# A decoder layer with product-key experts: one more raw weight buffer and half-row gather buffers in the first expert stage, a third pair buffer in the second

## The reference, cut to what matters

```python
def peer(a, w_q, k1, k2, u_exp, v_exp):        # 512 tokens, D = 2048, 8 heads, 16384 experts
    ...                                        # the routing: 16 experts and 16 gates per token and head
    def one(args):
        a_c, e_c, g_c = args
        u_sel = jnp.take(u_exp, e_c, axis=0)
        h = jnp.einsum('bthkd,btd->bthk', u_sel, a_c, preferred_element_type=jnp.float32)
        w = (g_c * jax.nn.gelu(h)).astype(a_c.dtype)
        v_sel = jnp.take(v_exp, e_c, axis=0)
        return jnp.einsum('bthk,bthkd->btd', w, v_sel)
```

## Time and profile before

| | |
|---|---|
| median of 3 runs | 2978.49 us (2977.01 to 2980.55) |
| profiled execution, its own time | 2979.05 us |
| its span in the profile | 2977.3 us |
| PE busy | 2923.9 us, 98% |
| DVE busy | 2259.8 us, 76% |
| POOL busy | 1440.4 us, 48% |
| ACT busy | 1268.4 us, 43% |
| moved by DMA | 843 MB, 283 GB/s on average |

### The profile page before, as it was taken

The page is one execution under the profiler, slowest core; times in us unless marked ns, Lnnn a source line. Parts: engine busy times, 40 slices in busy tenths (PEclk is TensorE's granted clock), DMA queues, the critical chain, the costliest instruction groups (busy, mean ns, idle before and its releaser), DMA issues.

```text
span 2977.3 us, 43219 instructions
## 1 busy us (share of the span) xinstructions
PE 2923.9 (98%) x16888; PEld 2739.3 (92%) x16888; DVE 2259.8 (76%) x2836; ACT 1268.4 (43%) x1898; POOL 1440.4 (48%) x859
## 2 busy tenths in 40 slices
PE   9999999999999999999999999999999999999998
PEld 7888668889999999999999999999999999999787
DVE  5466664578888877877787769888888889998545
ACT  5224541333333433333333344555555555566522
POOL 1012000008888778888888235443445778772000
PEclk9999999999999999999999999999999999999999
DMA  8469422235555599999999889999999999998222
GB/s 299 169 238 331 142 85 99 99 110 128 139 125 130 140 343 358 373 361 358 372 341 361 320 350 408 411 417 418 415 417 415 417 413 416 417 395 314 92 93 98
DMA packets 195807, 843.09 MB, mean 283 GB/s; under 512 B 66780, under 2 KB 87276, under 8 KB 116556
## 3 DMA queue, kind: packets, MB, share of 16 engines
q0 software_dynamic: 104592, 413.77, 37.9%
q1 hardware_dynamic: 72336, 404.83, 36.0%
q10 hardware_dynamic: 18732, 22.59, 2.2%
HBM read 768.01 MB, written 73.06 MB: 282 GB/s over the span
## 4 chain that ended last, share of the span: by engine, by line
PE 66%; DVE 13%; DMA 11%; POOL 5%; issue 3%; ACT 2%; SPq 0%; DVEq 0%; ACTq 0%; POOLq 0%
PE ps L1838 21%; PE ps L1836 21%; PE ps L1837 21%; DMA pair_in<-pair 7%; DVE wL L1110 4%; DVE rows L1617 3%; POOL pair_in L612 2%; DVE hT L1629 2%; POOL rows L597 1%; POOL rows L605 1%; DMA rows<-u_rows,idx_s 1%; DVE b_acc L1634 1%; ACT wH L656 1%; DMA rows<-v_rows,idx_b 1%; DMA raw<-s_v 1%
## 5 line engine op out<-in xcount | busy, mean ns | idle before, releaser
L1836 PE MATMUL ps<-aH,wH 128*128 128x344 f32 (+2 forms) x3088 | 1057.4, 342 | 6.3 <-DVE wL L1110 6.3
L1838 PE MATMUL ps<-aH,wL 128*128 128x344 f32 (+2 forms) x3088 | 1055.4, 342 | 0.0
L1837 PE MATMUL ps<-aL,wH 128*128 128x344 f32 (+2 forms) x3088 | 1047.1, 339 | 0.0
L565 POOL DMA_INDIRECT pair<-gates_r,idx_d x384 | 740.5, 1928 | 376.7 <-DVE gates_r L1525 242.5
L1110 DVE TENSOR_TENSOR wL<-raw,wH 128x2048 fp32r<-128x2048 f32 x333 | 778.1, 2337 | 183.2 <-ACT wH L656 180.8
L656 ACT ACTIVATE wH<-raw 128x2048 fp32r<-128x2048 f32 x333 | 636.3, 1911 | 591.5 <-PE ps L1838 538.6
L1836 PE MATMUL ps<-actH,wH 128*128 128x344 f32 x2048 | 656.7, 321 | 14.3 <-DVE wL L1110 13.8
L1838 PE MATMUL ps<-actH,wL 128*128 128x344 f32 x2048 | 656.1, 320 | 0.0
L1837 PE MATMUL ps<-actL,wH 128*128 128x344 f32 x2048 | 651.6, 318 | 0.0
L1836 PEld LDWEIGHTS ps<-aH,wH 128*128 128x128 f32 x3088 | 578.5, 187 | 47.1 <-DVE wL L1110 5.8
L1837 PEld LDWEIGHTS ps<-aL,wH 128*128 128x128 f32 x3088 | 580.6, 188 | 38.8 <-issue 1.0
(11 more groups left out here) (288 smaller groups left out, 2626.7 us busy)
## 6 DMA issues: line engine op xcount, KB each, us to landing
raw<-s_pu SPq DMA_DIRECT2D x128, 1024.0 KB
raw<-s_pv SPq DMA_DIRECT2D x128, 1024.0 KB
pair<-zeros POOLq DMA_DIRECT2D x44, 1024.0 KB, 8.7
pair_in<-pair SPq DMA_DIRECT2D x128, 348.0 KB
pair<-ut ACTq DMA_DIRECT2D x128, 172.0 KB
raw<-s_out SPq DMA_DIRECT2D x16, 1024.0 KB
raw<-s_pq SPq DMA_DIRECT2D x16, 1024.0 KB
raw<-s_gate SPq DMA_DIRECT2D x16, 1024.0 KB
```

The source lines that it names most:

```text
L565: pool.indirect_dma_start(out=gates_flat, out_offset=bass.IndirectOffsetOnAxis(ap=idx_d[0:m, t, c:c + 1], axis=0), in_=gates_r[0:m, t, c:c ...
L1836: mm(out, wh, xh, start=start, stop=False, skip_group_check=skip_group_check)
L1837: mm(out, wh, xl, start=False, stop=False, skip_group_check=skip_group_check)
L1838: return mm(out, wl, xh, start=False, stop=stop, skip_group_check=skip_group_check)
```

## The change

First stage: a fifth raw buffer, so that chunks 36 to 119 rotate through three; chunk 38 waits for a_tok_ready, as raw4 lies where gain_row did. The buffers of rows become eleven halves of 8 KB. The joined array uv_rows is gone: every pick has a gather_u and a gather_v of its own, each with its buffer and semaphore. The u halves of the first 64 picks use two buffers, the v halves three. POOL's loop is gather_u, two adds, gather_v, two adds. U_PICKS goes from 64 to 68, so that 64 picks are spread over the slots 36 to 117, four over the last eight, and 97 over the second stage.

Second stage: pair_in has three buffers, and SP issues each late chunk load one value load earlier. On ACT weight_hi comes before the weigh_pick of the slot.

```diff
-U_PICKS, LATE = 64, 4
+U_PICKS, LATE = 68, 4
...
+def halves_of(j):
+
+    if j < U_PICKS - LATE:
+        return j % 2, 2 + j % 3
+    if j < U_PICKS:
+        return 4, 2 + j % 2
+    if j <= MAIN:
+        return (5, 6) if (MAIN - j) % 2 else (7, 8)
+    return 9, 10
...
+FIRST_THIRD, END_THIRD = ROUTE_U + 4, KEYS - GROUP
...
+    if FIRST_THIRD <= c < END_THIRD:
+        return (0, 1, 4)[(c - FIRST_THIRD) % 3]
...
+def pair_at(c):
+
+    return c % 2 if c < GROUP else (c - GROUP) % 3
...
-            with sp.Fori(0, (KEYS - GROUP - ROUTE_U) // 2) as i:
-                for b in range(2):
-                    load(nu + ROUTE_U + 2 * i + b, stream["pu"][ROUTE_U + 2 * i + b, :, :], b)
+            for c in range(ROUTE_U, KEYS - GROUP):
+                if c == FIRST_THIRD + 2:
+                    sp.wait_ge(a_tok_ready, 1)
+                load(nu + c, stream["pu"][c, :, :], c % 2)
...
-            def gather(j):
-
-                if ROW_USED[j] >= 0:
-                    pool.wait_ge(pick_done, ROW_USED[j] + 1)
-                pool.indirect_dma_start(
-                    out=rows[ROW_AT[j]][:, :, :].rearrange("p a d -> p (a d)"), out_offset=None, in_=a["uv_rows"],
-                    in_offset=bass.IndirectOffsetOnAxis(ap=ids_of(j), axis=0)).then_inc(row_landed[ROW_AT[j]], 16)
+            def free_half(j, at):
+
+                dots_before, sums_before = free_of(j, at)
+                if dots_before:
+                    pool.wait_ge(dot_done, dots_before)
+                if sums_before:
+                    pool.wait_ge(pick_done, sums_before)
...
             for j in range(U_PICKS - LATE + 1):
-                gather(j)
+                gather_u(j)
                 if j >= 1:
-                    for n in range(added, min(added + 4, HEADS * NTD * TOPK)):
+                    for n in range(added, min(added + 2, HEADS * NTD * TOPK)):
+                        add_gates(n)
+                        added = n + 1
+                gather_v(j)
+                if j >= 1:
+                    for n in range(added, min(added + 2, HEADS * NTD * TOPK)):
                         add_gates(n)
                         added = n + 1
...
                 if not tail:
+                    c = GROUP * (g + 1) + q
+                    weight_hi(c, q, 1 - b, pre_in[pair_at(c)])
                     for o in range(v_step(g, q), v_step(g, q + 1)):
                         if o % 2 == 0:
                             weigh_pick(o // 2)
-                    weight_hi(GROUP * (g + 1) + q, q, 1 - b, pre_in[q % 2])
```

More of the change, by code:

```diff
@@ L130, in raw_at @@
 def raw_at(n):
-    v = n - S0["pv"]
+    c, v = n - S0["pu"] + ROUTE_U, n - S0["pv"]
+    if FIRST_THIRD <= c < END_THIRD:
+        return (0, 1, 4)[(c - FIRST_THIRD) % 3]
     return (v - 2) % 4 if 4 <= v < KEYS - GROUP else n % 2
+def pair_at(c):
+    return c % 2 if c < GROUP else (c - GROUP) % 3
+PAIR_PREV, PAIR_LANDED = [], []
+for _c in range(KEYS):
+    _same = [j for j in range(_c) if pair_at(j) == pair_at(_c)]
+    PAIR_PREV.append(_same[-1] if _same else -1)
+    PAIR_LANDED.append(16 * (1 + len(_same)))
 RAW_PREV, RAW_LANDED = [], []
@@ L226, in trunk_layer @@
     actL = [at(f"actL{i}", [GROUP, TA], R, ACT_AT[i] + 12 * KB) for i in range(2)]
-    rows = [at(f"rows{i}", [2, D], F, o) for i, o in enumerate((W0 + 32 * KB, W0 + 16 * KB, W0, A0, A0 + 16 * KB, W0 + 24 * KB))]
+    HALF_AT = [M0, M0 + 8 * KB, W0, W0 + 8 * KB, W0 + 16 * KB] + [A0 + 8 * KB * i for i in range(4)] + [W0 + 24 * KB, W0 + 32 * KB]
+    half_row = [at(f"half{i}", [D], F, o) for i, o in enumerate(HALF_AT)]
     gain_row = at("gain_row", [D], F, W0 + 24 * KB)
@@ L270, in trunk_layer @@
     idx_s = at("idx_s", [P], U32, C0 + 2 * KB + 1536)
-    pair_in = [at(f"pair_in{i}", [PW + TD], F, C0 + 4 * KB * i) for i in range(2)]
+    pair_in = [at(f"pair_in{i}", [PW + TD], F, C0 + o) for i, o in enumerate((0, 4 * KB, 7 * KB))]
     gate_in = [p[:, 0:TD] for p in pair_in]
@@ L310, in trunk_layer @@
         rows_loaded, perm_loaded = sem("rows_loaded"), sem("perm_loaded")
-        raw_loaded = [sem(f"raw_loaded{i}") for i in range(4)]
+        raw_loaded = [sem(f"raw_loaded{i}") for i in range(5)]
         hi_ready, lo_ready, tile_done = sem("hi_ready"), sem("lo_ready"), sem("tile_done")
@@ L335, in trunk_layer @@
         pre_stored = [sem(f"pre_stored{i}") for i in range(2)]
-        pair_loaded = [sem(f"pair_loaded{i}") for i in range(2)]
+        pair_loaded = [sem(f"pair_loaded{i}") for i in range(3)]
         g_scaled = sem("g_scaled")
@@ L347, in trunk_layer @@
             sem("gain_row_loaded"), sem("tok_done_h"), sem("tok_copied"), sem("a_tok_ready"))
-        row_landed = [sem(f"row_landed{i}") for i in range(6)]
-        v_row_landed = [sem(f"v_row_landed{i}") for i in range(3)]
+        half_landed = [sem(f"half_landed{i}") for i in range(11)]
         dot_done, dot_gelu, pick_weighed, pick_done = sem("dot_done"), sem("dot_gelu"), sem("pick_weighed"), sem("pick_done")
@@ L457, in load_late_chunk @@
             def load_late_chunk(v):
[L459 to L462, removed]
+                load_chunk(GROUP + v)
             for v in range(3):
@@ L621, in _ @@
             for c in range(GROUP):
-                apply_gates(c, c % 2)
+                apply_gates(c)
                 if c % 2 == 0 and U_PICKS - LATE + 1 + c // 2 < U_PICKS:
-                    gather(U_PICKS - LATE + 1 + c // 2)
+                    gather_u(U_PICKS - LATE + 1 + c // 2)
+                    gather_v(U_PICKS - LATE + 1 + c // 2)
             for j in range(U_PICKS, U_PICKS + 2):
```

73 lines of the change are left out of this document (37 added, 36 removed).

## The result

The changed kernel takes 3106.8 us (median of 4 runs, 3102.44 to 3110.39) against 2979.52 us for the kernel before in the same sessions: 1.0417 times as long, 95% interval 1.0398 to 1.0437. That is 127 us more; the forecast was 88 more (3067), in a range of 2995 to 3112. The profiled execution took 3105.07 us, its span is 3103.1.

What follows compares the result with a forecast made beforehand. POOL, issuing the indirect DMAs, was taken to bound the first stage, and DMA was a little short in the second. 2979.05 + 98 (first stage) - 10 (second stage) = 3067 us, range 2995 to 3112.

Steps and rivals of the forecast that it cites:

- What bounds: First stage: POOL, which issues every indirect DMA, has nearly nothing left; second stage: a little short of DMA, 413 GB/s.
- Part 1: First stage: splitting each gather adds a POOL instruction of 1.30 us; with stretch a pick costs POOL 11.6 us.
- Part 2: First stage: 68 picks ask for 9.70 us each, POOL needs 11.6; the stage gets 98 us longer.
- the 30 us that I kept to either side: First stage: margin around the 98 us lengthening, as the 0.67 us stretch averages 53 picks of all phases.
- Part 3: First stage: three raw buffers let SP load one chunk further ahead; nothing to plus 1 us.
- Part 4: Second stage: 97 picks in place of 101 and a third pair buffer; 10 us gained, between 14 gained and 10 lost.
- A: First stage: POOL keeps pace and the second gather costs nothing that shows; 2969 us, chance 0.06.
- B: First stage: the DMA rate becomes the bound if POOL is quicker than reckoned; 3003 us, chance 0.08.
- C: PE's clock falls in the gaps at every pick; 3143 us, chance 0.07 shared with stretches worse than reckoned.
- The signs to look for: Profile: POOL without gaps over 0.30 us to about 1720, 11 to 12.5 us a pick; second-stage PE gaps below 6 us.
- about 90: First stage: DVE waits for DMA by some 90 us, PE for wL by about as much between 1088 and 1730.
- The end of the stage near 1860: First stage: should end near 1860 in place of 1761.

Runs made afterwards that it cites:

- E6: Changed kernel with every second of the 228 gate adds in the loop left out: 2965.2 us, ratio 0.9940.
- E1: Changed kernel with U_PICKS back at 64, gathers still in halves: 3091.6 us, ratio 1.0356.
- E2: Kernel before with U_PICKS = 68 and nothing else, gathers joined: 3016.2 us, ratio 1.0102.
- E3: Kernel before with only the second-stage changes (three pair buffers, earlier chunk loads, weight_hi ahead of weigh_pick): 2980.2 us, ratio 0.9999.
- E5: Changed kernel, but the row add of the first 64 picks reads its third operand from PSUM instead of SBUF: 3069.8 us, ratio 1.0291.
- E4: E3 with 68 picks, gathers joined and two raw buffers: 3011.3 us, ratio 1.0099.
- E8: E3 (64 picks) with 162 gate adds ahead of the loop in place of 156, the rest spread evenly: 2998.8 us, ratio 1.0060.
- E11: Changed kernel with two raw buffers in the first stage in place of three: 3106.3 us, ratio 1.0414.
- E12: Changed kernel with two more matmuls at the head of each slot from chunk 40 on: 3132.2 us, ratio 1.0494.
- E7: E3 with 66 picks and 162 gate adds ahead of the loop in place of 156, the rest spread evenly: 2979.1 us, ratio 0.9975.
- E9: E3 with 66 picks, 156 gate adds first and the rest in groups that end with a head: 2978.5 us, ratio 0.9983.
- E10: E3 with 65 picks, 156 gate adds first and the rest in groups that end with a head: 2977.1 us, ratio 0.9983.

## Why the prediction was right, and where its sizes were off

The direction, the engine and the wait were right, and one term was mis-sized. That 3106.8 still lies inside the range, by 5 us, is partly luck: the first stage overran the bound of its own term (98 + 30 us), and 2979 + 128 - 10 would be 3097. The upper bound stood somewhat above that, and the second stage gave back 4 us more than forecast.

**What bounds.** Right in the first stage, open in part in the second. In the first POOL's list of instructions sets the pace (E6: take adds away and all gaps go; E1 and E2: six instructions a pick cost 110 us with the old plan, five cost 34 with the new one). In the second it is not the number of buffers, as E3 shows; that it is the bytes remains the likelier reading, not a shown one.

**Part 1, the price of a second gather, 1.30 us.** Right: 0.99 to 1.00 and 0.30 where nothing stretches it.

**Part 2, the stretch.** This is the term that was mis-sized. I carried 0.67 us for each DVE instruction with two SBUF inputs over to the changed kernel, 11.6 us a pick. Measured with the same sum it is 212 x (1.948 - 1.54) + 53 x 0.44 + 53 x 0.17 = 119 us over 69 lo and 54 row adds, 0.97 each, and 12.35 us a pick. 53 x 0.75 = 40 us, nearly the whole difference of 98 and 139.8: gather_u(57) was put at 1712.8 and came at 1749.3, 36.5 us later (2.3 of them from before the stage). The rest agrees: from there to the issue of the v half 8.4 us (5.7 forecast), to its landing 8.1 (7.0), row add and lo 4.5 (4.6). The bounds that I gave for this term (98 + 95) took it in, the 30 us that I kept to either side did not: forecast 98, measured 139.8. The argument for those 30 us, that 0.67 was an average over all phases of the engines, was the weak step: the change moved the phases.

Why the stretch grows can be read from two rows of POOL and one of DVE in the changed kernel:

```profile
1727.98 3.50 POOL L599 DMA_INDIRECT pair<-gates_r,idx_d  x1 [0.30 <-issue]
...
1735.33 3.20 POOL L599 DMA_INDIRECT pair<-gates_r,idx_d  x1 [0.30 <-issue]
```

```profile
1727.84 2.35 DVE L1668 SCALAR_TENSOR_TENSOR hT<-half,pick_w,hT 128x2048 f32<-128x2048 f32 x1 [3.88 <-issue]
...
1734.94 2.29 DVE L1150 TENSOR_TENSOR wL<-raw,wH 128x2048 fp32r<-128x2048 f32 x1
```

The adds begin 0.14 and 0.39 us into the DVE instruction, and so wait for nearly all of it. The kept traces can all be counted in one way: for each instruction of POOL that begins at least 0.05 us into a DVE instruction with two SBUF inputs, how far into it (gather of pick 4 to that of pick 57, some 120 meetings in each; 68 in E5, whose only such instruction is lo), beside the stretch for each such DVE instruction, reckoned as above.

| | begins after, us | stretch, us |
|---|---|---|
| E3 | 1.47 | 0.63 |
| kernel before | 1.43 | 0.68 |
| E4 | 1.36 | 0.74 |
| E2 | 1.27 | 0.85 |
| E8 | 1.25 | 0.85 |
| E1, changed kernel, E11, E12 | 1.13 to 1.15 | 0.96 to 0.98 |
| E5 | 0.80 | 1.25 |

The two add to about 2.1 us in every row, and in E7, E9 and E10 too (E6, whose POOL also waits for buffers, has 1.21 and 0.83). So what POOL pays is what is left of the DVE instruction when it comes, and in every kernel with halves it comes earlier than in those without. DVE was paced by PE before (it waited 121.5 us for it from 1050 to 1760) and is paced by POOL's own gathers now (19.5 us). That this coupling is the reason for the shift was not tried by itself. E2 and E4, where DVE waits for joined gathers, lie between; but their periods (10.8 and 10.6 us) stand against 10.54 in the kernel before and 10.36 in E3, whose first stage is the same, so 0.2 us of a period is scatter.

**Part 3**, nothing from the third raw buffer: right (E11).

**Part 4**, 10 us gained: measured 14.0, of which the gaps of the stage are 9.5. The other 4.5 us no row here places. Right in sign. Of its two causes the fewer picks count and the buffer hardly does: E1, with three buffers and 101 picks, has 13.2 us of gaps over the same 935 us.

**The rivals.** A had the right time for a kernel whose POOL has room (E6 is 2965, A said 2969). It did not come true, and with it the sentence of the Trainium skill that the prediction sets beside it (DMA: Bandwidth & Descriptors, Anatomy of one DMA: descriptor generation is a small, variable part) is answered for this case: an issue holds POOL for 1.00 us beside nothing and 1.44 us on average for a gather_u, and 64 more of them cost 95 us (E4 to the changed kernel). B did not appear. C's premise came true, at 0.94, and its price did not (E12); the row of tenths that spoke against it can't show such a fall.

**The signs to look for.** POOL without gaps to 1749: yes, but for 7.3 us, and 12.35 us lies inside the 11 to 12.5 that were named. PE dense behind pick 57, gaps of 4.15 us in the second stage (below 6 forecast), no waits for row buffers and no shorter adds: yes. PE's waits for wL from 1088 to 1749, its group by line:

```profile
L1875 PE MATMUL ps<-aH,wH 128*128 128x344 f32 x1121 | 377.6, 337 | 89.8 <-DVE wL L1150 89.7
```

That is 89.7 us against "about 90". But the stage lost 140, and the rest is in the mean of 337 ns, which was 320 for the same group before: PE's busy time over the span grew by 42 us. The end of the stage near 1860 was wrong by 41 us, for the stretch. And DVE's waits for rows, put at some 90 us, were more than twice that (from 1050 to 1760; the row add's wait has no releaser in the trace, and stands in its order where it waits for the v half):

```profile
DVE hT L1668 <- issue: 104.1, 38, 5.1
DVE half L1657 <- DMA half<-u_rows,idx_s: 104.0, 35, 6.5
```

DVE waited for PE 102 us less than before in that stretch: so much of the lateness had room on DVE, and only the rest reached PE.

## What to carry to other kernels

Count the instructions of the engine that issues the indirect DMAs against the period of the plan before splitting a transfer: an engine whose every gap is the same 0.30 us is full, though it is "48% busy" over the span. Price its instructions with what stretches them, and don't carry an average price over: it was 0.63 to 0.85 us with joined gathers and 0.97 with halves and all adds, as the change moved the moments at which the engines meet. And see where a serial wait falls in such a list: the same wait cost at most 3.8 us behind a gather and 5.3 to 9.2 us right behind the transfer that it waits for (kernel before and E8).

## What the runs showed of the hardware that I had not expected

The granted clock of TensorE fell in the stage in which PE had gaps at every pick (busy 492 of 568 us): 0.94 on average, 0.89 to 0.97 in stretches of 60 us from 1148 to 1740. These are means of its two levels, 2.4 and 1.2 GHz: at 0.94 the engine is at the lower one for an eighth of the time. Before the change the same stretch, without gaps, had 1.00. One such stretch of the changed kernel:

```profile
1200.00:1260.00 60.00, 51.70 (x286) 50.84 (x287) 38.42 (x28) 14.45 (x21) 51.15 (x30) 0.89 0.88 291
```

It cost nothing that shows there, as PE was waiting for others anyway (E12), but by its busy time, 42 us longer over the span, it moves that much out of PE's waits, so that PE's gaps alone understate what the stage lost. E2 shows the same on a smaller scale: 37 us of gaps, and a stage that ends 51 us later.
